# A hybrid decoder step: v projected in a sweep ahead of the tiles, i and g as three fp32r products in each tile, and some steps of a tile in another order

## The reference

```
mod = silu(c) @ w_ada + b_ada                       # 12 panels of 512 columns
h = rmsnorm(x, norm1) * (1 + sc1) + sh1
q, f_pre, i, g, v = split(h @ w_in)                 # 5 x 512 columns
f = lb + (1 - lb) * sigmoid(f_pre); logf = log(f); k = 1 - f; qa = silu(q)
# HGRN2, 4 heads of 128, in time order
S_t = diag(f_t) S_{t-1} + (1 - f_t) outer i_t;  o_t = S_t^T qa_t
o = rmsnorm_per_head(o) * hgrn_norm * silu(g)
# pooling, 4 groups of 128 channels, windows 2, 4, 8, 16
d = trailing_mean(v) - v;  y = (d @ w_pool[g]) * pool_scale
x = x + g1 * (concat(o, y) @ w_out)
h2 = rmsnorm(x, norm2) * (1 + sc2) + sh2
x = x + g2 * moe(h2)                                # top 4 of 32 experts
out = rmsnorm(x, final_norm)
```

## Time and profile before

| | us |
|---|---|
| median of three runs | 2159.7 |
| the profiled execution, whole | 2158.67 |
| its span in the trace | 2157.1 |
| PE busy | 2050.3 (95%) |
| DVE busy | 1534.7 (71%) |
| ACT busy | 1286.9 (60%) |
| POOL busy | 770.0 (36%) |
| mean granted TensorE clock | 0.974 of full |

### The profile page before, as it was taken

How to read it: one execution, slowest core, us unless ns; L and a number is a source line. 1 busy time by engine, 2 the same in 40 slices (tenths; PEclk the granted TensorE clock), 3 DMA queues, 4 the chain that set the end, 5 groups by cost and what they waited for, 6 DMA issues and landing times.

```text
span 2157.1 us, 38550 instructions
## 1 busy us (share of the span) xinstructions
PE 2050.3 (95%) x11946; PEld 1500.1 (70%) x11947; DVE 1534.7 (71%) x2050; ACT 1286.9 (60%) x1717; POOL 770.0 (36%) x997
## 2 busy tenths in 40 slices
PE   6998999999967899999999999999999999999995
PEld 5896676666646676677676668877686677788562
DVE  4533456666867677777786669988696797898557
ACT  3632344343416576676775667867686786888554
POOL 3224345555722232222242223432233243334124
PEclk9999999999968999999999999999999999999997
DMA  9667511121368788889886779999899899999765
GB/s 351 236 222 263 183 49 49 53 68 46 97 221 288 284 316 278 301 330 328 291 312 241 283 268 389 389 338 361 294 371 344 291 349 336 364 378 395 250 219 183
DMA packets 154531, 572.26 MB, mean 265 GB/s; under 512 B 22560, under 2 KB 41773, under 8 KB 120165
## 3 DMA queue, kind: packets, MB, share of 16 engines
q1 hardware_dynamic: 127405, 511.87, 62.8%
q0 software_dynamic: 25520, 56.53, 10.4%
q10 hardware_dynamic: 1552, 3.13, 0.4%
HBM read 521.36 MB, written 50.29 MB: 265 GB/s over the span
## 4 chain that ended last, share of the span: by engine, by line
PE 60%; issue 4%; ACT 3%; DVE 2%; ACTq 0%; DVEq 0%; DMA 0%; POOLq 0%
PE pg L2237 10%; PE pg L2238 9%; PE pg L2240 9%; PE py L2196 6%; PE py L2172 6%; PE py L2173 5%; PE py L2176 5%; PE pg L2210 3%; ACT hi L2374 3%; PE pt L2167 1%; PE pt L2161 1%; DVE lo L2466 1%; PE pg L2230 1%; PE pt L2182 0%; ACT L2389 0%
## 5 line engine op out<-in xcount | busy, mean ns | idle before, releaser
L2237 PE MATMUL pg<-hi,xs 128*128 128x512 f32 x1056 | 432.6, 410 | 0.0
L2238 PE MATMUL pg<-lo,xs 128*128 128x512 f32 x1056 | 411.9, 390 | 0.0
L2466 DVE TENSOR_TENSOR lo<-spare,hi 128x1024 fp32r<-128x1024 f32 x264 | 306.3, 1221 | 81.8 <-ACT hi L2374 78.8
L2466 DVE TENSOR_TENSOR lo<-w_out,hi 128x1024 fp32r<-128x1024 f32 x272 | 313.8, 1219 | 70.6 <-ACT hi L2374 69.4
L2240 PE MATMUL pg<-hi,xs 128*128 128x512 f32 x1056 | 325.7, 390 | 0.0
L2466 DVE TENSOR_TENSOR lo<-raw,hi 128x1024 fp32r<-128x1024 f32 x264 | 314.5, 1221 | 8.3
L2374 ACT ACTIVATE hi<-w_out 128x1024 fp32r<-128x1024 f32 x272 | 265.5, 1049 | 35.1 <-SPq L2004 27.6
L2374 ACT ACTIVATE hi<-spare 128x1024 fp32r<-128x1024 f32 x264 | 259.2, 1048 | 43.2 <-PE pg L2240 43.2
L2374 ACT ACTIVATE hi<-raw 128x1024 fp32r<-128x1024 f32 x264 | 270.4, 1056 | 23.4 <-PE pg L2240 23.4
L2237 PEld LDWEIGHTS pg<-hi,xs 128*128 128x128 f32 x1056 | 198.3, 188 | 71.6 <-issue 14.1
L2172 PE MATMUL py<-hi,aT 128*128 128x512 f32 x528 | 219.5, 416 | 9.0 <-DVE lo L2466 9.0
(11 more groups left out here) (484 smaller groups left out, 3537.2 us busy)
## 6 DMA issues: line engine op xcount, KB each, us to landing
w_out<-in_w_gu SPq DMA_DIRECT2D x136, 1024.0 KB, 7.2
spare<-in_w_gu SPq DMA_DIRECT2D x132, 1024.0 KB, 10.3
raw<-in_w_down SPq DMA_DIRECT2D x132, 1024.0 KB, 8.3
ada_w<-in_w_ada SPq DMA_DIRECT2D x4, 2048.0 KB
spare<-in_w_ada SPq DMA_DIRECT2D x4, 2048.0 KB
moe_rows<-small SPq DMA_DIRECT2D x9, 512.0 KB, 6.7
w_v<-in_w_in SPq DMA_DIRECT2D x2, 2048.0 KB, 17.2
w_i<-in_w_in SPq DMA_DIRECT2D x2, 2048.0 KB, 18.7
```

The source lines that it names most:

```text
L2237: pe.matmul(pg[u][b][:, :], xs[:, kt, 0, :], wh[:, u, :], start=False, stop=False)
L2238: pe.matmul(pg[u][b][:, :], xs[:, kt, 0, :], wl[:, u, :], start=False, stop=False)
L2466: dve.tensor_tensor(lo[q % RING][:, :, :], grain(q % GRAINS), hi[q % RING][:, :, :].bitcast(F32), ALU.subtract).then_inc(s["lo"], 1)
```

## The change

1. **v as a third panel of the sweep.** Its fp32 product in each tile goes. `block_fq` becomes `block_fqv`, and 16 units of v follow the 64 of f and q, in the order of chunks 2, 3, 0, 1. Chunks 2 and 3 are still in `hTc`; chunks 0 and 1 are read back from `h_tiles` (`refill`, 2 MB each), which now holds the high and the low part (1 MB a tile instead of 512 KB). v goes to DRAM and is loaded by tile (`load_v`) straight into `vx`. `high_raw` remains for the sample tokens alone.
2. **The last four modulation panels** stand within the sweep of v, after units 66, 69, 72 and 75 (`SWEEP_ADA`), each loaded into the same half of `spare`, so a panel's load starts when the one before has been used.
3. **i and g as three fp32r matmuls** per piece of depth (24 each per tile) from `hT2` and from the split weights `ig`, which ACT and DVE split during the sweep (`split_ig`).
4. **Order in a tile.** PE: i directly after `mix`, then `pooling`, ranks and `route_rows`, then g, with `transpose_o` within it. DVE: `norm_out` of tile t-1 before the norm of o, `h2_high` before `decays`. ACT: norm of the output before that of o, `o_cols` later, and the table for the square root is loaded before `k_rows`. POOL's order in a tile stays as it was.
5. The sample tokens' v comes from the sweep; for their i and g the weights are loaded again in tile 7.

The diff, cut to its core:

```diff
--- before.py
+++ after.py
+        SWEEP = (2, 3, 0, 1)
+        UNITS = [(c, panel, m) for c in range(CHUNKS) for panel in range(2) for m in range(H)] + [(c, 2, m) for c in SWEEP for m in range(H)]
+        F_DONE, AGAIN = BLOCKS_FQ - H, BLOCKS_FQ + 3 * H
+        SWEEP_ADA = [BLOCKS_FQ + 2 + 3 * j for j in range(len(PANELS) - BEFORE)]
             def panel(p):
                 j, n = place_of(p), PANELS[p]
                 if p >= EARLY:
-                    sp.wait_ge(s["ada_mm"], max(p - 1, EARLY))
-                    sp.wait_ge(s["modt"], max(p - 1, EARLY))
+                    done = p if p > BEFORE else max(p - 1, EARLY)
+                    sp.wait_ge(s["ada_mm"], done)
+                    sp.wait_ge(s["modt"], done)
...
             sp.wait_ge(s["u_mm"], BLOCKS_FQ)
+            panel(BEFORE)
+            for j in range(2):
+                sp.wait_ge(s[f"hT_out{j}"], 32 * CHUNKS // 2)
+
+            def refill(c, done):
+                sp.wait_ge(s["u_mm"], done)
+                for n in (2 * c, 2 * c + 1):
+                    part, at = part_of(n, P)
+                    sp.dma_start(part[:, :, :, at:at + P].bitcast(F32), scratch["hT"][n]).then_inc(s["h_back"], 16)
+
+            panel(BEFORE + 1)
+            refill(0, BLOCKS_FQ + H)
+            sp.dma_start(hT2[:, :, :, :].bitcast(F32), scratch["hT"][0]).then_inc(s["hT_in"], 16)
+            panel(BEFORE + 2)
+            sp.wait_ge(s["h_back"], 32)
+            refill(1, BLOCKS_FQ + 2 * H)
+            panel(BEFORE + 3)
+            sp.wait_ge(s["u_mm"], AGAIN)
             for j in range(USLOTS):
-                sp.wait_ge(s[f"u_out{j}"], stored(j, BLOCKS_FQ))
-            sp.wait_ge(s["hT_out"], 16 * (TILES + 1))
+                sp.wait_ge(s[f"u_out{j}"], stored(j, AGAIN))
+            sp.wait_ge(s["hTs_out"], 16)
             sp.sem_inc(s["ready"], 1)
...
-            def block_fq(n):
-                c, panel, m = n // (2 * H), n // H % 2, n % H
+            def block_fqv(n):
+                c, panel, m = UNITS[n]
                 N, bank, tiles = width(c), u_ps[n % 4], 2 * c + 2 + (c == CHUNKS - 1)
-                if n % (2 * H) == 0:
+                if n < BLOCKS_FQ and n % (2 * H) == 0:
                     pe.wait_ge(s["h_hi"], 2 * tiles)
                     pe.wait_ge(s["h_lo"], 2 * tiles)
+                if panel == 2 and c < 2 and m == 0:
+                    pe.wait_ge(s["h_back"], 32 * c + 32)
                 if n >= 4:
                     pe.wait_ge(s["u"], n - 3)
                 for kt in range(KT):
-                    if n in (0, H) and kt % 2 == 0:
+                    if n in (0, H, BLOCKS_FQ) and kt % 2 == 0:
                         pe.wait_ge(s["fq_hi"], panel * 4 + kt // 2 + 1)
                         pe.wait_ge(s["fq_lo"], panel * 4 + kt // 2 + 1)
-                    wh, wl = (fq[:, panel, part, kt, m * P:(m + 1) * P] for part in range(2))
+                    wh, wl = (fq[:, panel % 2, part, kt, m * P:(m + 1) * P] for part in range(2))
                     hh, hl = (hTc[c % 2][:, kt, part, 0:N] for part in range(2))
                     pe.matmul(bank[:, 0:N], wh, hh, start=(kt == 0), stop=False)
                     pe.matmul(bank[:, 0:N], wh, hl, start=False, stop=False)
                     last = pe.matmul(bank[:, 0:N], wl, hh, start=False, stop=(kt == KT - 1))
                 last.then_inc(s["u_mm"], 1)
 
-            def project_v(t, src):
-                for m in range(H):
-                    for kt in range(KT):
-                        last = pe.matmul(X3[:, m * P:(m + 1) * P], w_v[:, kt, m * P:(m + 1) * P], src[:, kt * P:(kt + 1) * P],
-                                         start=(kt == 0), stop=(kt == KT - 1))
-                last.then_inc(s["v_mm"], 1)
-
-            def rows(bank, w, src, name):
-                for kt in range(KT):
-                    last = pe.matmul(bank[:, :], src[:, kt * P:(kt + 1) * P], w[:, kt, :], start=(kt == 0), stop=(kt == KT - 1))
-                last.then_inc(s[name], 1)
+            def rows(bank, j, kts):
+                for kt in kts:
+                    hh, hl = (hT2[:, kt, part, :] for part in range(2))
+                    wh, wl = (ig[:, j, part, kt, :] for part in range(2))
+                    pe.matmul(bank[:, :], hh, wh, start=(kt == 0), stop=False)
+                    pe.matmul(bank[:, :], hh, wl, start=False, stop=False)
+                    last = pe.matmul(bank[:, :], hl, wh, start=False, stop=(kt == KT - 1))
+                if kts[-1] == KT - 1:
+                    last.then_inc(s[("i_mm", "g_mm")[j]], 1)
 
...
-                    if first_tile(t) and j in TILE_ADA:
-                        ada(BEFORE + TILE_ADA.index(j))
                 transpose_k(t, P, T0)
                 mix(t, P, LV)
-                pooling(t, P)
-                pe.wait_ge(s["gs"], t + 1)
-                pe.wait_ge(s["hT_in"], t * 16 + 16)
-                project_v(t + 1, hT)
-                transpose_o(t, P)
-                pe.wait_ge(s["pool_y"], t + 1)
-                rows(X2, w_i, hT, "i_mm")
+                pe.wait_ge(s["hT_in"], t * 16 + 32)
+                rows(X3, 0, range(KT))
+                if back:
+                    pe.wait_ge(s["x1"], t)
+                pooling(t, P, X0)
                 if back == 2:
-                    pe.wait_ge(s["x1"], t)
                     rank(t - 2, P, X1)
                 if back:
-                    pe.wait_ge(s["oT"], t + 1)
                     route_rows(t - 1, P)
-                pe.wait_ge(s["vx"], t + 2)
-                rows(X3, w_g, hT, "g_mm")
+                pe.wait_ge(s["gs"], t + 1)
+                rows(X2, 1, range(KT - 3))
+                transpose_o(t, P, L0)
+                rows(X2, 1, range(KT - 3, KT))
                 if back:
                     pe.wait_ge(s["S"], t + 2)
                     route_logits(t - 1, P)
...
                         transpose_h(TILES, NS)
                     if (c, m) == AHEAD_ADA[0]:
-                        pe.wait_ge(s["h_raw"], 4)
+                        pe.wait_ge(s["h_hi"], 4)
+                        pe.wait_ge(s["h_lo"], 4)
                     if (c, m) in AHEAD_ADA:
                         ada(EARLY + AHEAD_ADA.index((c, m)))
-            pe.wait_ge(s["w_v_in"], 48)
-            project_v(0, x)
+            for n in range(BLOCKS_FQ, len(UNITS)):
+                block_fqv(n)
+                if n in SWEEP_ADA:
...
+            def split_ig(j, u):
+                cut = slice(2 * u, 2 * u + 2)
+                if j == 0:
+                    act.wait_ge(s["w_i_in"], 32)
+                    act.wait_ge(s["u_mm"], BLOCKS_FQ)
+                else:
+                    act.wait_ge(s["w_g_in"], 16)
+                    act.wait_ge(s["ig_lo"], u + 1)
+                act.activation(ig[:, j, 0, cut, :], (w_i, w_g)[j][:, cut, :], ACT.Copy).then_inc(s["ig_hi"], 1)
...
-                    if first_tile(t) and i in TILE_MOD:
-                        store_mod(BEFORE + TILE_MOD.index(i))
+                act.activation(rs[0:NS, 0:1], eps[0:NS, :], ACT.Sqrt)
                 k_rows(t, P, T0)
-                norm_o(t, P)
                 if back:
                     norm_out(t - 1, P)
+                norm_o(t, P)
                 log_f(t + 1, P)
                 decays(t + 1, P)
                 for i in range(PRE):
                     act.dma_start(h2[:, :], a["norm2"].broadcast_to([P, D])).then_inc(s["rows2"], 16)
                     for dst, m in adds[2:]:
                         load_row(dst, m, "rows2")
-                keep_v(t + 1)
-                o_cols(t, P)
                 keep_i(t + 1)
                 if back:
                     h2_low(t - 1, P)
+                o_cols(t, P, L0)
                 gate_g(t + 1)
...
+            def split_ig(j, u):
+                cut = slice(2 * u, 2 * u + 2)
+                dve.wait_ge(s["ig_hi"], j * 4 + u + 1)
+                dve.tensor_tensor(ig[:, j, 1, cut, :], (w_i, w_g)[j][:, cut, :], ig[:, j, 0, cut, :].bitcast(F32), ALU.subtract).then_inc(s["ig_lo"], 1)
+
+            def keep_u(n):
+                c, panel, m = UNITS[n]
+                N = width(c)
+                dve.wait_ge(s["u_mm"], n + 1)
+                dve.wait_ge(s[f"u_out{n % USLOTS}"], stored(n % USLOTS, n))
+                dve.tensor_copy(ust[:, n % USLOTS, 0:N], u_ps[n % 4][:, 0:N]).then_inc(s["u"], 1)
...
             def residual(t, j):
                 if back:
                     residual(t - 1, 1)
                 carry_state(t)
+                if back:
+                    norm_out(t - 1, P)
                 norm_o(t, P)
-                pool_scaled(t, P)
+                pool_scaled(t, P, X0)
+                if back:
+                    h2_high(t - 1, P)
                 decays(t + 1, P, P)
                 for i in range(PRE):
                     border(t + 1, P, i, BLOCKS[i])
                     dve.wait_ge(s["rows2"], 16 * 4)
```

(10 more changed lines are left out.)

289 lines of the change are left out of this document (154 added, 135 removed).

## The result

Before: 2159.64 us (median of 4 runs, 2158.58 to 2159.95). After: **2194.93 us** (median of 4, 2191.42 to 2196.09). The ratio is 1.0163, 95% interval 1.015 to 1.0176: 1.6% slower. The profiled execution of after took 2196.09 us, its span is 2194.5: +37.4 on that of before, where the sum said +23.9.

A forecast was written before the change was run, and what follows sets the result against it. PE was taken to bound the tiles before the change, POOL's chain after it. Terms of +41.6, -6.6, -1.0, -6.5, -1.9 and -1.7 sum to +23.9 on 2158.67: 2182 us, likeliest range 2168 to 2196, 8-in-10 range 2162 to 2198.

The forecast's parts named there:

- POOL thus starts at +15.1: In each tile, counted from its transposes of k, T(t): POOL's unbroken stretch starts at +15.1 us, not +11.9.
- Operands of levels 1 and 2: POOL's four operations in a tile get cheaper away from DVE's norm: 2.9 us in place of 4.5.
- I add 1.7: Slow PE clock behind the wait before level 3 costs 1.7 us per interval, making 49.4 us for 49.86.
- PE idle 8 us: In each steady tile PE stands still for 8 us before level 3, waiting for POOL.
- T(6) to T(7): Interval between these tiles' transposes of k: sample tokens' v goes, levels still wait for POOL; -1.7 us (-3.4 to +1).
- Before T(0): Stretch before tile 0's transposes of k, now with the sweep of v and four panels: 88.7 us for 47.05, +41.6.
- The gap in the sweep of f and q: The 4.42 us gap before tile 3's transposes and the slow clock behind it go: -6.6 us (0 to -7).
- T(0) to T(1) and T(1) to T(2): First two tile intervals: -1.0 us (-4 to +2), waiting for modulation rows; -6.5 us (-7.5 to -4.5), without `list_slots`.
- A: Rival: the tiles follow PE, each of seven intervals loses 9.9 us; 2119 us, chance 0.08.
- B: Rival: POOL's chain binds but starts at +11.9 as before, and the clock holds; 2155 us, chance 0.08.
- C: Rival: the sweep starves with stalls of 9 us and the clock suffers more; 2202 us, chance 0.12.
- D: Rival: the clock holds at gaps of 8 us; 2174 us, chance counted within the forecast's 0.68.

The follow-up runs named there:

- a_lists: Changed kernel with the indirect DMAs of `list_slots` and the wait for their landing moved to the start of POOL's stretch: 2163.97 us, ratio 1.0027.
- a_decays: Changed kernel with the next tile's decays and borders moved on DVE ahead of `pool_scaled` and the copy of h2: 2178.05 us, ratio 1.0088.
- a_logits: Changed kernel with the copy of the router's logits moved on DVE ahead of `place`: 2202.44 us, ratio 1.021.
- b_lists: Kernel before the change, with `list_slots` moved on POOL in the same way as in a_lists: 2159.9 us, ratio 1.0009.
- a_norm: Changed kernel with its part that norms the routed rows ahead of o undone: 2177.33 us, ratio 1.0095.
- a_fill_again: Changed kernel with 24 unread products added on PE before level 3 in tiles 2 to 6, second measurement: 2190.17 us, ratio 1.0152.
- a_again: The changed kernel unaltered, measured once more on the same chip as a_fill_again: 2200.5 us, ratio 1.0195.
- a_three: Changed kernel with the moves of a_lists, a_decays and a_logits together, panels at their old places: 2146.12 us, ratio 0.9938.

## Why the prediction was right, and where its sizes were off

Right in mechanism: PE's work fell by 9.9 us a tile, and the tiles kept their pace because POOL's stretch, started later by the new order on DVE, releases level 3. a_lists, a_decays and a_logits each altered one link of that chain, and the intervals and waits moved as it says, though not each total; b_lists shows that the link was slack before. The step "POOL thus starts at +15.1" measured +14.9, "the end is +33.1" +32.9, level 3 "at +34.7" +34.9 (T(4) to T(5)).

That the total came out as near as +37.4 for +23.9 is partly luck. The stretches up to T(7), all that was added up, gave +42.5, 18.6 us more than forecast; the stretch from T(7) on, taken as unchanged, gave 5.1 back for no known reason. The measured 2194.9 lies at the upper end of "2168 to 2196", and the same kernel measured again took 2200.5, above even the 2198 of the 8-in-10 range. The terms, one by one:

- **Operands of levels 1 and 2**, 2.9 us in place of 4.5: 3.2 (464.99 to 468.21). Cheaper, as said, though 0.85 each and not 0.72. a_norm brought 1.30 back beside the norm. By the rule that was weighed (the Trainium skill, SBUF — State Buffer, Who interferes with whom) this is what should happen, and the traces agree: 1.30 beside the norm, 0.85 away from it.
- **The clock, "I add 1.7"**: the term that was mis-sized most in the interval. In the four intervals of after it measured 2.3, 2.6, 2.9 and 3.0, on average 2.7, and I had read it from one gap of 3.39 us, with no stretch that showed one of 6 to 8. The table of waits under a_fill_again shows that a gap of 3 us could as well have read nothing or 2.9. With 2.7 the interval is 50.4; measured were 50.65 to 51.09. Over four intervals this term is 4.0 of the 5.9 by which they missed; most of the rest is level 3 at +35.1 on average.
- **PE idle 8 us**: 1.67 at level 1 and 6.41 at level 3. That part of it would move to level 1, since `weigh` gets dear beside POOL's operands, I had not seen; a_logits shows that it does not set the interval while POOL binds.
- **T(6) to T(7)**, -1.7, measured +3.1. Two causes. `listed`, which waits for the landing of the lists, was costed at nothing. In the loop POOL stands 0.45 us at that place; here 3.91, and only then come the operands of level 3. The weights loaded again, 4 MB, were on their way just before (253 GB/s from 579 to 585 us); that they held the lists up fits, but no run shows it:

```profile
583.66 1.28 POOL L1736 TENSOR_TENSOR gs<-gs,hnorm 128x512 f32<-128x512 f32 x1
588.86 0.30 POOL L1682 TENSOR_SCALAR rows_s<-rows_s 128x128 f32<-128x128 f32 x1 [3.91 <-DMA slots<-entry,slotc]
```

  The rest, 1.0, is the clock: PE waited 10.18 us, and from level 3 to T(7) it took 21.6 us, not 20.6. Before, the wait at that place was 1.18 us and POOL's 2 us of room hid it. I had asked what would be late next inside the loop, and not at its end. a_lists moved the lists, and there this wait is gone.
- **Before T(0)**, +41.6, measured +49.0, the largest miss. Up to level 0 it was 75.0 us for 70.1. The waits for panels were 6.9 us, where I took 4 (0 to 9 were the bounds). Of the other 2, 1.1 is the second panel, which took 3.06 us behind its wait where the others take 1.95: the granted clock of 180.96 to 195.83 is 0.89, and 1.00 in the rest of the sweep of v. The levels of tile 0 took 21.05 for 18.6, at a granted clock of 0.72: with the panels gone from them, PE waited 5.38 us before level 3, POOL being in its unbroken stretch with `windows` in it, and ran slowly behind. I had subtracted the panels' 7.6 us from the levels as if they hid nothing. Before, two of them stood ahead of level 3 while POOL was still busy: its stretch ended 4.8 us behind level 0, and in after 7.5 us. PE's waits that were left before were put down to DVE's takes.
- **The gap in the sweep of f and q**, -6.6, measured -8.0, with no wait but one of 0.56 us left in it. In the nine other profiles the first panel comes 0.3 to 4.3 us later, and the gain is that much smaller.
- **T(0) to T(1) and T(1) to T(2)**: -0.3 for -1.0 (the modulation rows landed at T+28.2, not +26.5) and -5.3 for -6.5 (behind the 3.17 us wait the loss was 1.7, where I took half of that; a_again lost 2.9 there and a_logits 0.3).

The rivals: A (the tiles follow PE) is not what the change does, but a_three makes it nearly true with three moves, and goes to 41.4 us an interval. B's lever is real: with the start at T+12.0 (a_decays) the time was 17 us under that of after, where B had 19. It was 2178 and not 2155, since it came off 2195 and not 2182, and since B's other 8 us, for a clock that holds, did not come: the wait was still over 5 us and the loss behind it 2.8 to 3.1. C's stalls were 7 of its 9 us. D (the clock holds at gaps of 8 us) did not come in any interval with a wait over 5 us.

## What to carry to other kernels

When one engine's work is shortened, follow every other engine's in-order stretch to the point where the first one needs it, and ask what in it has no reason to stand ahead of that. Here 5 us of DMA issues stood there, free while the engine had 2 us of room and 7.4 us per tile once it had none. A wait on TensorE can cost more than its length: add the slow stretch behind it, read from several gaps of about the same size, since one gap says little (0.1 to 2.9 us behind waits of 3 us here). And work that is taken out of a stretch with waits in it is not worth its own duration there.

## What the runs showed that was not expected

- DVE's tiny operations pay for POOL's long ones. Four `tensor_scalar` of 32 columns took 3.48 us in after, 0.87 each, which is one POOL operand (0.85). The same four took 2.38 in a_decays and 1.27 beside POOL's windows in a_norm, and a like four (at 479.11 in after), while POOL issued its lists, 0.68 in all. The same page and section of the Trainium skill lists `tensor_scalar` among the operations that can take the port pair shared with GpSimd, and says that whichever instruction comes first has the pair for its whole length and the other blocks; these times fit that, and no run tests it by itself.
- 24 products of 128x512 in each of five tiles, whose results nobody reads, made the kernel 10.3 us faster than the one without them, on the same chip.
- The same kernel at two times: 2194.9 and 2200.5 us, with before within 2 us both times. A change of 0.3% in a kernel with waits is told only beside its control, and what an edit did in the tiles is told better by the stretch T(0) to T(7) than by the total.
